# Prompt mixing rebuilt: four tiles projected at once in split fp32r, through DRAM, with key and query norms as scalars

## The chip, the cores and the metric

The kernel runs on one core of a Trainium2 chip. The time is that of one execution on the device, in microseconds (us). TensorE is called PE here (its weight loads PEld), VectorE DVE, ScalarE ACT, GpSimd POOL; SP is the engine that issues the DMAs.

## The reference, cut to what matters

One layer is computed for 2048 prompt positions and for 8 short running streams with the same weights. Here it is the mixing of the prompt that matters:

```python
h = rms_norm(x, norm1)
p = h @ w_in                      # 1024 -> 3080: u_A v_A q k v_B z (512 each), beta 4, a 4
y_a = gmlp_spatial(gelu(u_a), gelu(v_a), ...)        # 4 groups, blocks of 128 positions, then a norm per group
qkv_c = silu(causal_conv(qkv))    # depthwise, width 4
q = l2norm(q) * DK ** -0.5        # 4 heads of 128
k = l2norm(k)
g = -exp(a_log) * softplus(a + dt_bias); beta = sigmoid(b)
o, S = gated_delta_chunked(q, k, v, g, beta, S0, chunk)  # S_t from S_{t-1}: the tiles follow one another
y_b = rms_norm(o, gdn_norm) * silu(z)
x = x + concat(y_a, y_b) @ w_o    # from here on: the output phase
x = x + (silu(h2 @ w_gate) * (h2 @ w_up)) @ w_down
```

In a chunk the delta rule needs the inverse of a unit lower triangular matrix T, whose entries are beta, a decay exp(b_i - b_j) and k_i . k_j.

## The kernel before

Three stages follow one another: `mix_phase` for the sample streams, `mix_phase` for the prompt (16 tiles of 128 positions), `out_phase` (output projection and feed-forward, with every fp32 operand split into two fp32r halves and each product made of three). The first two keep the whole of w_in in SBUF (`w_in_sb`); `out_phase` takes the same region over.

In `mix_phase` each engine executes its own list, written out by hand, with semaphores between them; every engine executes strictly in its order. `tile(m, par, project, fronts)` handles tile m's recurrence and, in pieces between its products, the projection of tile m + 1: `qkv_columns`, `va_columns`, `z_columns`, `u_columns`, `gate_columns` (L960, L986 and L950), products in plain fp32 with 128 moving columns (512 for va). Per tile these are 160, 8 and 8. `project` is off for the last tile alone. Tiles 1 to 13 run in a loop of two tiles a turn.

A tile runs so on PE. `start` (L1011, L1012) sums the decays over partitions in fp32r with the constants `after_r` and `ones_r`, and likewise the squares of k and q. ACT turns these into `decay`, `eb`, `r_k` and `r_q` with Exp and Ln (L457 to L470), DVE makes the normalised `kn` and `qn` (L693, L695). `products` turns v and k to rows (L1043, L1048) and forms k . k and k . q (L1052, L1057); DVE makes `mt`, the masked matrix, of them (L708). Six doubling levels then build the inverse X and its transpose (`level_lx` L1081, `level_xlx` L1095 and L1099), each with a copy on ACT (L491), two updates on DVE (L735, L742) and a masked copy on POOL (L376). `scan` solves for delta (L1148), `outputs` and `state` follow, and `out_norm` (L1189) sums the squares of the output over partitions. ACT makes a reciprocal root of that sum, and DVE the scaled output. Between them ACT changes its function table (ACT_TABLE_LOAD): Silu, Gelu, and Exp with Ln lie in three different sets.

The convolution is done on DVE per tile in pieces of 128 columns (`conv_tap`, L677 and L679), and DVE splits the squares into halves (L755).

## Time and profile before

| | |
|---|---|
| time, median of 3 runs (lowest to highest) | 3163.26 us (3154.65 to 3163.99) |
| profiled execution: its span; its own time is not listed apart | 3160.3 us |
| PE busy, PEld, DVE, ACT | 97%, 91%, 44%, 30% of the span |
| sample mixing, prompt mixing, output phase | to 135.5, to 1361.8, to 3160.3 us |
| granted PE clock, mean | 0.982 of full |

The span runs from the first to the last instruction; the median of the runs is 2.96 us above it. Busy time says what an engine executed, not what it was waited for: for that one reads the instructions in order of time and looks at what ended the idle time before each. A 128-column fp32 product shows as two records, so "x16" of them are eight products. The ends of PE's records are modelled and overlap the next one's start; what a product costs is the distance between starts.

### The profile page before, as it was taken

How to read it: one execution, taken by the hardware profiler on the slowest of the kernel's cores; microseconds unless marked ns; L12 is line 12 of the kernel's file. 1: busy time of each engine (PE TensorE's matmuls, PEld its weight loads, DVE VectorE, ACT ScalarE, POOL GpSimd, SP SyncE). 2: the span in 40 equal slices, each digit the busy share in tenths (PEclk: the TensorE clock that was granted, in tenths of full speed). 3: DMA queues.
4: the chain of work that ended last, by engine and by line, in shares of the span. 5: the costliest groups of instructions: out<-in, count | busy, mean ns of one | idle time of the engine just before them, and what ended most of it. 6: DMA issues, size and time to landing. Idle time of an engine off the chain costs nothing.

```text
span 3160.3 us, 49318 instructions
## 1 busy us (share of the span) xinstructions
PE 3059.0 (97%) x20376; PEld 2869.0 (91%) x20376; DVE 1395.4 (44%) x2574; ACT 951.1 (30%) x1598; POOL 160.4 (5%) x155
## 2 busy tenths in 40 slices
PE   7799999999999999989999999999999999999998
PEld 6599999999899999879999999999999999999998
DVE  3255555454554554535343333453333435444344
ACT  3133433344443343324112112332112114322222
POOL 2001111111111111100000000000000000000000
PEclk9699999999999999989999999999999999999999
DMA  5100000000000000142221221521222215222220
GB/s 203 56 8 15 15 15 14 15 14 15 28 15 15 14 14 8 68 130 67 67 66 53 66 66 53 174 76 58 66 63 66 58 53 174 81 80 71 75 80 33
DMA packets 188615, 182.15 MB, mean 58 GB/s; under 512 B 5697, under 2 KB 162438, under 8 KB 188473
## 3 DMA queue, kind: packets, MB, share of 16 engines
q1 hardware_dynamic: 188472, 180.01, 18.3%
q8 instruction: 120, 1.97, 0.3%
q14 instruction: 23, 0.18, 0.0%
HBM read 159.37 MB, written 20.61 MB: 57 GB/s over the span
## 4 chain that ended last, share of the span: by engine, by line
PE 53%; DVE 2%; ACT 1%; issue 1%; DMA 0%; DVEq 0%; POOL 0%; ACTq 0%; POOLq 0%
PE gate_ps L1751 6%; PE gate_ps L1753 6%; PE gate_ps L1752 6%; PE up_ps L1751 6%; PE up_ps L1752 6%; PE up_ps L1753 6%; PE down_ps L1752 5%; PE down_ps L1751 5%; PE down_ps L1753 5%; DVE w_in_sb L1690 0%; ACT h_hi L1584 0%; DVE w_in_sb L1745 0%; DVE w_in_sb L1684 0%; DMA w_in_sb<-mixed_tiles 0%; ACT h_hi L1549 0%
## 5 line engine op out<-in xcount | busy, mean ns | idle before, releaser
L960 PE MATMUL pr_p<-hT_p,w_in_sb 128*128 128x128 f32 x5120 | 646.2, 280 | 0.8 <-DVE hT_p L618 0.8
L960 PEld LDWEIGHTS pr_p<-hT_p,w_in_sb 128*128 128x128 f32 x5120 | 608.5, 194 | 5.2 <-DVE hT_p L618 1.2
L1751 PE MATMUL gate_ps<-h_hi,w_hi 128*128 128x384 f32 (+1 forms) x1056 | 345.8, 327 | 3.7 <-DVE h_lo L1696 3.5
L1753 PE MATMUL gate_ps<-h_hi,w_lo 128*128 128x384 f32 (+1 forms) x1056 | 345.5, 327 | 0.0
L1752 PE MATMUL gate_ps<-h_lo,w_hi 128*128 128x384 f32 (+1 forms) x1056 | 345.3, 327 | 0.0
L1751 PE MATMUL up_ps<-h_hi,w_hi 128*128 128x384 f32 (+1 forms) x1056 | 344.3, 326 | 0.0
L1752 PE MATMUL up_ps<-h_lo,w_hi 128*128 128x384 f32 (+1 forms) x1056 | 344.0, 326 | 0.0
L1753 PE MATMUL up_ps<-h_hi,w_lo 128*128 128x384 f32 (+1 forms) x1056 | 344.0, 326 | 0.0
L1634 DVE TENSOR_TENSOR w_in_sb<-up_ps,w_in_sb 128x384 f32<-128x384 f32 (+1 forms) x132 | 70.7, 535 | 598.1 <-PE up_ps L1753 598.1
L1646 DVE TENSOR_TENSOR w_in_sb<-down_ps,w_in_sb 128x1024 f32<-128x1024 f32 x187 | 228.7, 1223 | 182.8 <-PE down_ps L1753 182.8
L1751 PE MATMUL down_ps<-wd_hi,act_hi 128*128 128x512 f32 x748 | 291.6, 390 | 2.2 <-DVE w_in_sb L1646 2.2
L1752 PE MATMUL down_ps<-wd_lo,act_hi 128*128 128x512 f32 x748 | 291.7, 390 | 0.0
L1753 PE MATMUL down_ps<-wd_hi,act_lo 128*128 128x512 f32 x748 | 291.6, 390 | 0.0
L1541 ACT ACTIVATE act_hi<-w_in_sb 128x384 fp32r<-128x384 f32 (+1 forms) x132 | 67.1, 508 | 530.2 <-DVE w_in_sb L1634 530.2
L1624 DVE TENSOR_TENSOR w_lo<-w_in_sb,w_hi 128x2048 fp32r<-128x2048 f32 x78 | 178.5, 2289 | 63.9 <-ACT w_hi L1530 63.9
L1751 PEld LDWEIGHTS gate_ps<-h_hi,w_hi 128*128 128x128 f32 x1056 | 199.4, 189 | 5.6 <-issue 4.4
L1752 PEld LDWEIGHTS gate_ps<-h_lo,w_hi 128*128 128x128 f32 x1056 | 199.3, 189 | 1.2
L1753 PEld LDWEIGHTS gate_ps<-h_hi,w_lo 128*128 128x128 f32 x1056 | 199.1, 189 | 0.0
L1751 PEld LDWEIGHTS up_ps<-h_hi,w_hi 128*128 128x128 f32 x1056 | 198.3, 188 | 0.0
L1752 PEld LDWEIGHTS up_ps<-h_lo,w_hi 128*128 128x128 f32 x1056 | 198.3, 188 | 0.0
L1753 PEld LDWEIGHTS up_ps<-h_hi,w_lo 128*128 128x128 f32 x1056 | 198.3, 188 | 0.0
L376 POOL TENSOR_TENSOR lt_p<-mt_p,link 128x512 f32<-128x512 f32 x96 | 137.5, 1439 | 1061.4 <-DVE mt_p L708 725.9
(370 smaller groups left out, 4661.5 us busy)
## 6 DMA issues: line engine op xcount, KB each, us to landing
w_in_sb<-in_w_gate SPq DMA_DIRECT2D x66, 512.0 KB, 3.9
w_in_sb<-in_w_up SPq DMA_DIRECT2D x66, 512.0 KB, 5.2
w_in_sb<-in_w_down SPq DMA_DIRECT2D x33, 1024.0 KB, 4.9
w_in_sb<-in_w_o SPq DMA_DIRECT2D x24, 512.0 KB, 6.4
w_in_sb<-in_w_in SPq DMA_DIRECT2D x5, 2048.0 KB, 15.7
w_in_sb<-mixed_tiles SPq DMA_DIRECT2D x17, 512.0 KB, 4.2
out<-w_in_sb SPq DMA_DIRECT2D x17, 512.0 KB, 4.1
xf_p<-in_x_prompt SPq DMA_DIRECT2D x16, 512.0 KB, 4.4
```

The source lines that it names most:

```text
L376: pool.tensor_tensor(lt[:, l % 2], mt[:], over_heads(sh["link"][:, l + 1, :]), ALU.mult)\
L960: last = pe.matmul(bank_[:, c * P:(c + 1) * P], sh["w_in"][:, k, col + c * P:col + (c + 1) * P], hT[:, par, k], start=(k == 0), stop=(k == ...
L1541: act_e.activation(act_hi[:, c, h * half:(h + 1) * half], act[:, h, 0:half], ACT.Copy)\
L1624: dve.tensor_tensor(w_lo[:, c], wraw[:, c], w_hi[:, c].bitcast(F32), ALU.subtract)\
L1634: dve.tensor_tensor(act[:, h, 0:half], up_ps[h][:, 0:half], gate_act[:, h, 0:half], ALU.mult)\
L1646: dve.tensor_tensor(acc[:, t, :], down_ps[t % 2][:].rearrange("p a b -> p (a b)"), acc[:, t, :], ALU.add).then_inc(added[t], 1)
L1751: pe.matmul(out, w_h, x_h, start=start, stop=False)
L1752: pe.matmul(out, w_h, x_l, start=False, stop=False)
L1753: return pe.matmul(out, w_l, x_h, start=False, stop=stop)
```

## The change

`mix_phase` is kept for the sample streams. The prompt gets a function of its own, `prompt_phase`. All loops in it are written out.

- The projection goes by items: one of 25 blocks of 128 columns of w_in (`ORDER`), for four tiles at a time (`MACRO`), with 512 moving columns. An item is 8 blocks of the inner dimension times three fp32r products (`three`), and stands in four quarters (`quarter`). The weights are not kept: SP loads each block again for each round of four tiles (100 loads of 512 KB), ACT makes the high half, DVE the low half. The normalised input of the round, hT, is split once per round (`split_h`). The 8 gate columns are the last 128 columns of w_in, as an item.
- ACT copies an item's result out of PSUM. Convolution is done on 512 positions at once, with 3 carried over in `halo`. SP stores each result to a DRAM tensor `stream_tiles`, and loads it back per tile: 20 blocks as `rc`, in two buffers, the four of z as `z`, in one.
- A slot is one tile of the recurrence (slots 0 to 15), with 25 quarters between its steps. Four slots, -4 to -1, come first with quarters alone; the items end with slot 11, so slots 12 to 15 have none.
- SiLU and GELU are applied to the loaded streams at the end of a slot, for the next tile (`silu_z`, `silu_streams`, `gelu_streams`).
- The key norm is folded into scalars per row: four squares with sums on ACT (`key_norms`), its inverse into beta, its root into the rows of v. The query norm is folded into the norm of the output: the squares of q times a constant are added by one product to the sum of the output's squares. The four sums of squares of k and q before, and the normalised kn and qn, go.

```diff
+STREAMS = [(x, c) for x in ("k", "q", "v", "va", "u", "z") for c in range(4)]
+ORDER = [("k", 0), ("ba", 0), ("k", 1), ("u", 0), ("k", 2), ("u", 1), ("k", 3), ("va", 0), ("q", 0), ("u", 2), ("q", 1),
+         ("va", 1), ("q", 2), ("va", 2), ("q", 3), ("va", 3), ("v", 0), ("v", 1), ("v", 2), ("v", 3), ("u", 3),
+         ("z", 0), ("z", 1), ("z", 2), ("z", 3)]
+MACRO = 4
+EARLY = 20
+RING_W = 3
...
+            def load_weights(n):
+                if n < ITEMS:
+                    past(sp, s["w_lo_ready"], n - 1)
+                    col = column[ORDER[n % NI]]
+                    sp.dma_start(wraw[:, n % 2], w_dram[:, :, col:col + P]).then_inc(raw_loaded[n % 2], 16)
+
...
+            def quarter(n, part):
+                if part == 0:
+                    load_weights(n + 3)
+                if part == 3:
+                    if 1 <= n <= ITEMS and kind(n - 1) == "plain":
+                        store_stream(n - 1)
+                    if 2 <= n <= ITEMS + 1 and kind(n - 2) == "conv":
+                        store_stream(n - 2)
...
+            def split_weights(n):
+                if n < ITEMS:
+                    act.wait_ge(raw_loaded[n % 2], 16 * (n // 2 + 1))
+                    past(act, s["item_done"], n - RING_W + 1)
+                    act.activation(w_hi[:, n % RING_W], wraw[:, n % 2], ACT.Copy).then_inc(s["w_hi_ready"], 1)
+
+            def split_h(j):
+                past(act, s["item_done"], j * NI)
+                for k in range(KC):
+                    act.wait_ge(s["hraw_ready"], 2 * MACRO * (j + 1))
+                    act.activation(hT_hi[:, k], hraw[:, k], ACT.Copy).then_inc(s["hT_hi_ready"], 1)
...
+            def quarter(n, part):
+                if part == 0 and n % NI == 0 and n < ITEMS:
+                    split_h(n // NI)
+                if part == 1:
+                    split_weights(n + 2)
+                if part == 2 and 1 <= n <= ITEMS:
+                    keep_item(n - 1)
...
+            def silu_streams(t):
+                act.wait_ge(rc_loaded[t % 2], 16 * (t // 2 + 1))
+                act.activation(rc[:, t % 2, 0:12], rc[:, t % 2, 0:12], ACT.Silu).then_inc(s["silu_ready"], 1)
+
+            def silu_z(t):
+                act.wait_ge(z_loaded, 16 * (t + 1))
+                act.activation(z[:], z[:], ACT.Silu).then_inc(s["z_ready"], 1)
+
+            def gelu_streams(t):
+                act.activation(rc[:, t % 2, 16:20], rc[:, t % 2, 16:20], ACT.Gelu_apprx_tanh).then_inc(s["u_ready"], 1)
+                act.wait_ge(s["va_turned"], t + 1)
+                past(act, s["sa_pe"], t)
+                act.activation(va[:], gs_cols, ACT.Gelu_apprx_tanh).then_inc(s["va_ready"], 1)
...
+            def key_norms(t):
+                act.wait_ge(s["k_turned"], t + 1)
+                past(act, s["root_k_ready"], t)
+                for h_ in range(H_B):
+                    if h_ > 0:
+                        act.wait_ge(s["ssk_ready"], t * H_B + h_)
+                    act.activation(junk[:], heads[1][:, h_], ACT.Square, accum_out=k_norm[:, 0, h_:h_ + 1])\
+                       .then_inc(s["ssk_ready"], 1)
+                act.wait_ge(s["ssk_ready"], (t + 1) * H_B)
+                act.activation(k_norm[:, 1], k_norm[:, 0], ACT.Ln, bias=sh["eps"][:]).then_inc(s["ln_k"], 1)
+                act.wait_ge(s["ln_k"], t + 1)
+                past(act, s["beta_n_ready"], t)
+                act.activation(k_norm[:, 2], k_norm[:, 1], ACT.Exp, scale=-1.0).then_inc(s["inv_k_ready"], 1)
...
+            def slot(t):
+                j = (t + MACRO) // MACRO
+                if t >= 0:
+                    decays(t)
+                    upto(t, 2)
+                    key_norms(t)
+                    upto(t, 4)
+                    scaled_values(t)
+                    query_squares(t)
+                    upto(t, 7)
+                    copy_x(t)
...
+                upto(t, SLOT)
+                if t >= 0:
+                    act.preload_act_table_set("silu_and_others")
+                    silu_z(t)
+                if t + 1 >= 0 and t + 1 < TILES:
+                    silu_streams(t + 1)
+                    gelu_streams(t + 1)
+                exp_and_ln()
...
+            def three(out, w_h, w_l, x_h, x_l, start, stop):
+                pe.matmul(out, w_h, x_h, start=start, stop=False)
+                pe.matmul(out, w_h, x_l, start=False, stop=False)
+                return pe.matmul(out, w_l, x_h, start=False, stop=stop)
+
+            def quarter(n, part):
+                if n >= ITEMS:
+                    return
+                if part == 0:
+                    pe.wait_ge(s["w_lo_ready"], n + 1)
+                    if n >= 2:
+                        what = {"conv": "kept", "ba": "ba_ready", "plain": "plain_ready"}[kind(n - 2)]
+                        pe.wait_ge(s[what], nth(n - 2) + 1)
+                w = n % RING_W
+                for k in (2 * part, 2 * part + 1):
+                    if n % NI == 0:
+                        pe.wait_ge(s["hT_lo_ready"], KC * (n // NI) + k + 1)
+                    last = three(pr[n % 2][:], w_hi[:, w, k], w_lo[:, w, k], hT_hi[:, k], hT_lo[:, k],
+                                 k == 0, k == KC - 1)
+                if part == 3:
+                    last.then_inc(s["item_done"], 1)
+
...
+            def slot(t):
+                j = (t + MACRO) // MACRO
+                if t >= 0:
+                    decays(t)
+                    upto(t, 1)
+                    turn_keys(t)
+                    upto(t, 2)
+                    keys_keys(t)
+                    upto(t, 3)
+                    turn_values(t)
+                    keys_queries(t)
+                    upto(t, 6)
+                if (t + MACRO) % MACRO == 1 and j < MACROS:
...
+                for l in range(LV):
+                    upto(t, 8 + 2 * l)
+                    if t >= 0:
+                        level_lx(l, t)
+                        if l == 0:
+                            keys_state(t)
+                    upto(t, 9 + 2 * l)
+                    if t >= 0:
+                        level_xlx(l, t)
+                        if l == 1:
+                            gmlp_norm(t)
+                    if l in (1, 3) and fronted(t) is not None:
+                        turn_h(l // 2, fronted(t))
+                upto(t, 21)
+                if t >= 0:
+                    solve(t)
+                    upto(t, 22)
+                    outputs(t)
+                    state(t)
+                    upto(t, 24)
+                    output_norm(t)
+                upto(t, SLOT)
+                if 0 <= t + 1 < TILES:
+                    turn_va(t + 1)
+
+            pe.wait_ge(s["set_masks"], 1)
+            for m in range(MACRO):
+                turn_h(0, m)
+                turn_h(1, m)
...
-            mix_phase(nc, shared, dict(
-                x=x_prompt, y=scratch[0:n_prompt], new_gdn=gdn_prompt[0, 0], new_conv=conv_prompt[0, 0],
-                ahead=loads_ahead(bufs, x_tiles, scratch, w_o), **weights), False)
+            prompt_phase(nc, shared, region, dict(
+                x=x_prompt, y=scratch[0:n_prompt], new_gdn=gdn_prompt[0, 0], new_conv=conv_prompt[0, 0], rec=streams,
+                ahead=loads_ahead(bufs, x_tiles, scratch, w_o), **weights))
```

At the end of a tile and the start of the next PE's list before holds this (`pr` are projection banks, `gb` banks of the recurrence, `ones` the constant that sums the squares of the output in X):

```order
L939 MATMUL pr_p<-ident,staging_p 128x128 x4
L960 MATMUL pr_p<-hT_p,w_in_sb 128x128 x8
L1189 MATMUL gb_p<-X_p,ones 128x512
...
L939 MATMUL pr_p<-ident,staging_p 128x128 x4
L960 MATMUL pr_p<-hT_p,w_in_sb 128x128 x8
...
L1011 MATMUL gb_p<-g_upto_p,after_r 128x512
L1012 MATMUL gb_p<-g_upto_p,after_r 128x512
...
L960 MATMUL pr_p<-hT_p,w_in_sb 128x128 x17
```

After the change, from slot 2 to slot 3 (`gb_p<-g_upto_p` are the decays, `gs_p<-ident` the turn of va, the last row the turn of the keys):

```order
L2291 MATMUL gb_p<-sq_q_p,eps_q_p 128x512
L2293 MATMUL gb_p<-X_p,ones 128x512
L2113 MATMUL pr_p<-hT_hi_p,w_hi_p 128x512
L2114 MATMUL pr_p<-hT_lo_p,w_hi_p 128x512
L2115 MATMUL pr_p<-hT_hi_p,w_lo_p 128x512
...
L2170 MATMUL gs_p<-ident,w_in_sb 128x128 x4
L2174 MATMUL gb_p<-g_upto_p,after_r 128x512
...
L2113 MATMUL pr_p<-hT_hi_p,w_hi_p 128x512
L2114 MATMUL pr_p<-hT_lo_p,w_hi_p 128x512
...
L2188 MATMUL gb_p<-ident,w_in_sb 128x128 x4
```

Two quarters of six split products, one on either side of the turn of va and the decays, stand where a column block (x8), the square sums and 32 column products with 8 gate products between them stood ahead of the first turn.

ACT's list at the same place before, from the reciprocal root of the output's squares on:

```order
L457 ACTIVATE r_k_p<-gb_p,eps 128x512
L460 ACTIVATE r_k_p<-r_k_p 128x512
L452 ACT_TABLE_LOAD
L452 ACTIVATE u_p<-pr_p 128x512
L394 ACT_TABLE_LOAD
L467 ACTIVATE decay_p<-gb_p 128x512
L470 ACTIVATE eb_p<-gb_p 128x512
```

and after, from slot 2 to slot 3 (the first row ends that root, then a weight split and a copy out of PSUM, then z, the twelve blocks of k, q and v, then u and va):

```order
L1720 ACTIVATE r_p<-r_p 128x512
L1647 ACTIVATE w_hi_p<-w_in_sb 128x1024
L1661 ACTIVATE w_in_sb<-pr_p 128x512
L1825 ACT_TABLE_LOAD
L1708 ACTIVATE z_p<-z_p 128x512
L1704 ACTIVATE w_in_sb<-w_in_sb 128x1536
L1711 ACT_TABLE_LOAD
L1711 ACTIVATE w_in_sb<-w_in_sb 128x512
L1714 ACTIVATE va_p<-gs_p 128x512
L1641 ACT_TABLE_LOAD
L1725 ACTIVATE decay_p<-gb_p 128x512
L1728 ACTIVATE eb_p<-gb_p 128x512
```

The squares' roots r_k and r_q leave; the silu of all streams and a table load more now stand between the root and the exponentials of the decays.

## Rows read from the trace of the kernel before

**Rows 1.** The page: span of the execution

```profile
span 3160.3 us, 49318 instructions
```

**Rows 2.** The stage: busy us of PE, PEld, DVE, ACT, POOL; granted clock, DMA

```profile
135.47:1361.76 1226.29, 1184.99 (x9424) 1100.59 (x9424) 607.95 (x1717) 482.36 (x980) 141.91 (x105) 0.98 0.06 19
```

**Rows 3.** POOL in order of time: first mask product, tiles 1 and 14

```profile
282.86 1.68 POOL L376 TENSOR_TENSOR lt_p<-mt_p,link 128x512 f32<-128x512 f32 x1 [42.94 <-DVE mt_p L708]
...
1251.46 3.46 POOL L376 TENSOR_TENSOR lt_p<-mt_p,link 128x512 f32<-128x512 f32 x2 [42.86 <-DVE mt_p L708]
```

**Rows 4.** PE in order of time inside a tile: start, us, what

```profile
741.27 1.95 PE L960 MATMUL pr_p<-hT_p,w_in_sb 128*128 128x128 f32 x16
743.05 1.00 PE L1095 MATMUL gb_p<-LX_p,XT_p 128*128 128x64 f32 x8
743.90 1.05 PE L1099 MATMUL gb_p<-XT_p,LX_p 128*128 128x64 f32 x8
```

**Rows 5.** PE in order of time, end of a tile and start

```profile
787.22 1.02 PE L1189 MATMUL gb_p<-X_p,ones 128*128 128x512 f32 x2
788.08 0.60 PE L939 MATMUL pr_p<-ident,staging_p 128*128 128x128 f32 x4
...
790.22 0.48 PE L1011 MATMUL gb_p<-g_upto_p,after_r 128*128 128x512 f32 x1
790.54 0.40 PE L1012 MATMUL gb_p<-g_upto_p,after_r 128*128 128x512 f32 x1
...
801.55 0.60 PE L1043 MATMUL gb_p<-ident,silu_v_p 128*128 128x128 f32 x4
```

**Rows 6.** PE in order of time, split products of the output phase

```profile
2160.57 0.39 PE L1751 MATMUL down_ps<-wd_hi,act_hi 128*128 128x512 f32 x1
...
2171.90 0.39 PE L1753 MATMUL down_ps<-wd_hi,act_lo 128*128 128x512 f32 x1
```

**Rows 7.** ACT in order of time around the end of a tile

```profile
788.34 0.69 ACT L457 ACTIVATE r_k_p<-gb_p,eps 128x512 f32<-128x512 f32 x1 [2.13 <-PE gb_p L1189]
...
789.71 1.28 ACT L452 ACT_TABLE_LOAD   x1
791.00 0.60 ACT L452 ACTIVATE u_p<-pr_p 128x512 f32<-128x512 f32 x1
```

**Rows 8.** Order of time, the last tile, with no projection beside it

```profile
1306.73 1.02 PE L1189 MATMUL gb_p<-X_p,ones 128*128 128x512 f32 x2
...
1315.59 1.12 PE L1048 MATMUL gb_p<-ident,knq_p 128*128 128x128 f32 x4 [1.80 <-DVE knq_p L693]
...
1318.46 1.13 DVE L708 SCALAR_TENSOR_TENSOR mt_p<-gb_p,beta_p,decay_p 128x128 f32<-128x128 f32 x4 [0.26 <-PE gb_p L1052]
...
1335.45 1.04 PE L1196 MATMUL pr_p<-ident,tails_p 128*3 128x128 f32 x8
...
1336.76 1.00 PE L1081 MATMUL gb_p<-X_p,lt_p 128*128 128x64 f32 x8
...
1353.29 1.08 PE L1189 MATMUL gb_p<-X_p,ones 128*128 128x512 f32 x2
...
1361.76 0.10 POOL L1516 MEMSET eps_b<- 128x1 f32 x1 [22.58 <-POOLq L87]
```

**Rows 9.** Granted clock (eighth value) in 2 us pieces of that tile

```profile
1314.00:1316.00 2.00, 0.41 (x2) 0.41 (x3) 0.69 (x1) 1.94 (x4) 0.00 (x0) 0.65 0.67 223
...
1324.00:1326.00 2.00, 2.00 (x17) 2.00 (x16) 1.07 (x2) 0.21 (x1) 0.10 (x1) 0.79 1.04 413
```

**Rows 10.** Group by line and shape: a 1024-element DVE operation

```profile
L1668 DVE TENSOR_TENSOR h_lo<-w_in_sb,h_hi 128x1024 fp32r<-128x1024 f32 x17 | 20.8, 1223 | 15.5 <-ACT h_hi L1549 15.4
```

**Rows 11.** PE in order of time, the start of the stage

```profile
142.47 1.11 PE L939 MATMUL pr_p<-ident,staging_p 128*128 128x128 f32 x4 [14.08 <-DVE staging_p L611]
...
146.27 1.01 PE L960 MATMUL pr_p<-hT_p,w_in_sb 128*128 128x128 f32 x3 [0.78 <-DVE hT_p L618]
```

**Rows 12.** DMA issues: KB each, median us to landing

```profile
xf_p<-in_x_prompt SPq DMA_DIRECT2D x16, 512.0 KB, 4.4
```

More of the change, by code:

```diff
@@ L1299, in _, with stream_columns @@
                 turn_tails()
+def stream_columns():
+    names = [("k", 2 * D_A + D_B), ("q", 2 * D_A), ("v", 2 * D_A + 2 * D_B), ("va", D_A), ("u", 0), ("z", 2 * D_A + 3 * D_B)]
+    return {(x, c): col + c * P for x, col in names for c in range(4)}
+STREAMS = [(x, c) for x in ("k", "q", "v", "va", "u", "z") for c in range(4)]
+ORDER = [("k", 0), ("ba", 0), ("k", 1), ("u", 0), ("k", 2), ("u", 1), ("k", 3), ("va", 0), ("q", 0), ("u", 2), ("q", 1),
+         ("va", 1), ("q", 2), ("va", 2), ("q", 3), ("va", 3), ("v", 0), ("v", 1), ("v", 2), ("v", 3), ("u", 3),
+         ("z", 0), ("z", 1), ("z", 2), ("z", 3)]
@@ new lines, with prompt_buffers @@
+MACRO = 4
+EARLY = 20
+RING_W = 3
+def prompt_buffers(region):
+    KC = D_MODEL // P
+    flat = region[:].rearrange("p c n -> p (c n)")
+    taken, views = 0, {}
+    for name, shape, axes in (
+            ("hraw", (KC, MACRO * P), "p (a b) -> p a b"),
+            ("wraw", (2, KC, P), "p (a b c) -> p a b c"),
+            ("cin", (2, 4 + MACRO * P), "p (a b) -> p a b"),
+            ("conv", (2, MACRO * P), "p (a b) -> p a b"),
+            ("plain", (2, MACRO * P), "p (a b) -> p a b"),
+            ("ba", (MACRO * P,), None),
+            ("xf", (D_MODEL,), None),
+            ("h", (D_MODEL,), None),
+            ("spare", (504,), None),
+            ("rc", (2, EARLY, P), "p (a b c) -> p a b c"),
+            ("yT", (KC, P), "p (a b) -> p a b"),
+            ("lt", (2, H_B, P), "p (a b c) -> p a b c"),
+            ("LX", (LEVELS_OF[P], H_B, P), "p (a b c) -> p a b c"),
+            ("kq_eb", (2, H_B, P), "p (a b c) -> p a b c"),
+            ("v_rows", (H_B, P), "p (a b) -> p a b"),
+            ("k_dec", (H_B, P), "p (a b) -> p a b")):
+        n = math.prod(shape)
+        view = flat[:, taken:taken + n]
+        if axes:
+            view = view.rearrange(axes, **dict(zip("abcd", shape)))
+        views[name] = view
+        taken += n
+    return views
@@ L1857, in _, with stream_step @@
                     block_of(b, g, gi, n)
-def stream_step(nc, t, outs, scratch):
+def stream_step(nc, t, outs, scratch, streams):
     y_prompt, y_sample, gdn_prompt, conv_prompt, gdn_sample, conv_sample, v_sample = outs
@@ L1903 @@
     scratch = nc.dram_tensor("mixed_tiles", (tiles, P, D_MODEL), F32, kind="Internal").ap()
-    stream_step(nc, tensors, outs, scratch)
+    streams = nc.dram_tensor("stream_tiles", (SEQ // P, P, len(STREAMS) * P), F32, kind="Internal").ap()
+    stream_step(nc, tensors, outs, scratch, streams)
     result = run_bass_kernel_spmd(nc, [arrays], core_ids=[0]).results[0]
```

746 lines of the change are left out of this document (added).

## The prediction

> **What bounds the kernel now.** I first read the page for the span, 3160.3 us [rows 1], then split it by stages. Prompt mixing runs from 135.47 to 1361.76, 1226 us, and PE is busy for 1185 of them at 0.98 of full clock; DVE has 608, ACT 482 [rows 2]. What comes before and after is not touched, so only these 1226 us can move. PE bounds them: the pace of a tile is (1251.46 - 282.86) / 13 = 74.5 us [rows 3], and in the order of time one group of products starts where the last ends: eight 128-column products take 1.78 us (741.27 to 743.05), four 64-column ones 0.85 [rows 4], a 512-column fp32 product 0.86 (787.22 to 788.08) [rows 5]. So the question is what PE executes afterwards, and where it starts to wait.
>
> **PE's own work.** Projection of one tile before: 160 products at 0.22 = 35.6, eight of 512 columns at 0.86 = 6.9, eight small ones for the gates at 0.14 to 0.22, together about 44 us, 703 for 16 tiles. After: 100 items (four rounds of 25 column blocks) of 24 split products with 512 columns. The output phase has just these, 50 in 2171.90 - 2160.57 = 11.33, 0.227 each [rows 6]: 5.44 us an item, 544 in all. That is 159 us less. The rest of a tile, added up for the new order: 17 groups of the solve at 0.86, 14.7; six groups of four 128-column products at 0.89, 5.3; eight for the output, 1.8; six times four transposes at 0.45 (0.60 in [rows 5] with the modelled drain), 2.6; six fp32r products of 512 columns, 1.6; two fp32 ones for the output norm, 1.7. That is 27.7 us, and before it was 27.9 by the same prices (the four square sums go, one fp32 product for the query norm comes). A quarter item follows fp32 work some 21 times a slot, and the first fp32r product after fp32 took 0.32 against 0.227 [rows 5, 6]: 1.9 us a slot. A slot with projection beside a tile is therefore 25 x 1.36 + 1.9 + 27.7 = 63.6 us of dense PE. Were that all, twelve such slots would give back 131 us. It isn't all, in three places.
>
> **The start of a slot.** In the new order PE has, after the product that sums the output squares (call its end T), one quarter item, a turn, the two decays, one quarter item, and then the turn of the keys: 1.4 + 0.45 + 1.0 + 1.4 = 4.3 us. That turn waits for silu and for eb, the exponential of the second decay product. Before, PE had from 788.08 to 801.55, 13.5 us of work, between that sum and the first product that waits on the decays [rows 5]. What ACT does between T and eb, in its order: 0.26 until Ln starts (788.08 to 788.34) and 1.37 for Ln and Exp [rows 7]; splits and copies of two quarters, 0 to 1.65, mean 0.8; a table load 1.30 (789.71 to 791.00); silu of z 0.6; silu of 1536 elements, 1.5 as an estimate from 0.60 for 512 at 0.83 per thousand more; a table load 1.30; gelu of u and of v, 1.1; a third load 1.30; two exponentials, 1.1. Sum 10.7. PE idles 10.7 - 4.3 = 6.4 us, twelve times, 77 us. No other engine can hide it, since PE executes in order, and behind the turn stand all the slot's items.
> The row shows a table load of 1.28 us with the next operation 0.01 behind it [rows 7]. The Trainium skill (ScalarE: Activation LUTs, What ACT_TABLE_LOAD costs) puts some 1380 ns of drain beside the 1283 of the load, 2.66 us a switch. By its figure three loads a slot would add 4.1 us to each of sixteen slots, 66 us. The trace has the load's length but no drain, and I take the row.
>
> **The clock.** In the last tile PE had 0.41 us of work in 1314 to 1316 and its granted clock fell (0.65 of that piece at full), and was back only in 1324 to 1326 (0.79) [rows 9], 1.2 GHz in between. At the start of the stage dense work began at 146.27 [rows 11]. An idle stretch of 6.4 us is longer than that one, so I let the clock fall at each slot's start. Dense PE gets it back sooner than the sparse last tile did; I take 4.6 us at half speed, which costs 2.3, with 0 and 5 (the whole 10 us of that row) as bounds. Twelve slots: 28 us.
> Slots 4 and 8 also split a new round of h just there (eight ACT passes of 0.6, DVE behind each with 0.7, after DVE's masked decay and its product of 1024 elements, 1.22 [rows 10]): the first quarter waits until T + 12.6, an idle 9.7 in place of 6.4; slot 0 likewise, 75 us. In slots 1, 5 and 9 the gate sums wait for DVE, which takes the gates after gmlp: 2 us each. Slots 8 to 11 turn no h, 0.9 less each.
>
> **No cover in the last four tiles.** Before, one tile ran without projection: 1306.73 to 1353.29, 46.6 us [rows 8], against 27.7 of work. Now there are four, since items end after slot 11. Such a tile changes so: the keys are turned at T + 9.9 (the sum above without the 0.8) where 1315.59 is T + 8.0 (T = 1306.73 + 0.86), +1.9; the masked key products began 2.9 later (1318.46) [rows 8] and now wait for four squares with sums, Ln and Exp on ACT and beta on DVE, about 4.2, +1.3; a second fp32 product in the output norm, +0.9; twelve turns of tails go, -1.3 (1335.45 to 1336.76). 49.4 us, four times 198.
>
> **The sum.** The first tile's h is with PE at 142.47, 7.0 after the stage began, of which 4.4 is a landing [rows 11, 12]; three more tiles cost 4.4 + 2.6 each, turning 3.8 (to 146.27), the first split 1.3: 168.5. Then 25 items alone: 136, with four turned tiles 3.5, a cold start 2.3, gates 0.7: 311. Slots 0 to 11: nine at 63.6 + 6.4 + 2.3 = 72.3, one 75, two 75.6, + 6 - 3.5: 879, ends at 1190, its T at 1189. Four bare tiles: 1387. From T to the first instruction of the output phase as before, 1361.76 - 1354.15 = 7.6 [rows 8]: 1394.5, 33 us later than 1361.76. Span 3160.3 + 33 = 3193; the runs' median, 3163.26, is 3.0 above the profiled span, which holds for both: **3196 us**.
> The total agrees: 544 of items, 16 x 27.7 of tiles less 4 of turned h, 23 of switches, 92 of waits at starts and gates, 28 of clock, 4 x 21.7 of idle in bare tiles, 33 before the first item, 3 of its cold start and gates, 7.6 at the end: 1257 against 1226, +31. (Before, the same prices give 1188 of the 1226; the rest is edges of its loop and waits that I don't price, and is no term of the new sum.)
> Edits costed at nothing, with their cover: splitting weights (ACT 1.05, DVE 1.22 [rows 10]) and convolution (four DVE passes, 2.9) per item, 4.1 of DVE against 5.44 alone and 10 to 11 beside a tile; if a DVE pass were 40% longer the first round would be bound by it, +25. Weight blocks of 512 KB are issued about seven quarters before ACT needs them, 9.5 us in the first round, against 4.4 landing for the same size [rows 12]; streams go out at 256 KB an item and come back as 1.3 MB a tile, asked for some 12 us or more before use.
>
> **Rivals.** (1) The wait at the slot's start is covered, and PE is simply dense: it decides if ACT reaches eb within 4.3 us of T. Then 12 x 8.7 = 104 go: 3092, faster. For it speaks PE's 97% now; against it that ACT's list is strict and each length measured. 9%. (2) The waits come, but the clock stays up: -28, 3168, no change. The granted clock did fall in the last tile, yet behind a longer sparse stretch. 11%. (3) SP is the late one: it issues in order, and its waits for the taps of an item two back stand ahead of the next weight load; DVE passes those taps only after eb. If weights come late by one landing a slot less the slack, some 4 us: +48, 3244. Against: seven quarters of lead. 13%. (4) A switch of tables holds ACT for longer than its row, for a second time the 1.28 us of [rows 7]: three a slot, sixteen slots, +61, 3257. The row speaks against it, 0.01 us from the load's end to the next operation. 3%. The rule that would give it is the one of ScalarE: Activation LUTs in the Trainium skill, named above. My forecast, waits at the slots' starts and bare tiles as summed, holds 64%.
>
> **Numbers.** Own range of the forecast 3165 to 3230: clock 0 to 5 a slot (-28, +32), switches 0 to 23, bare tiles +-3 each. A difference under 0.3% (9.5 us, 3153.8 to 3172.7) can't be told from none here. Slower: 57 of the forecast's 64, all of (3), (4): 73. Same: 5 of the forecast, 7 of (2): 12. Faster: 2 of the forecast, 4 of (2), (1): 15. For 8 in 10 the range runs from 3140 to 3250: it leaves out (1), (4) and a little at both ends.
>
> **What the profile would show.** Right: split products 0.227 apart; an idle of PE of about 6 us ended by ACT's eb in each of slots 0 to 11, PEclk under 1.0 behind it; a pace of 72 to 73 us; four tiles near 49 us at the end; the output phase beginning near 1394. Wrong: PE waiting for the low half of the weights (then 3), no idle at the turn of the keys (1), an idle over 9 us there (4).

## The result, and the profile after

The changed kernel takes 3187.47 us (median of 4 runs, 3186.41 to 3196.89), the one before 3163.62 (4 runs on the same chip, 3154.65 to 3166.32): 1.0093 times as long by the estimate over all runs, 95% interval [1.0078, 1.0108]; the two medians alone give 1.0075. It is slower, by more than 0.3%. The profiled span grew from 3160.3 to 3184.9, by 24.6 us; 33 were forecast.

The page of the kernel after: the span, and the weight blocks' loads, which are new in this stage.

```profile
span 3184.9 us, 41999 instructions
...
w_in_sb<-in_w_in SPq DMA_DIRECT2D x100, 512.0 KB, 4.4
```

The mixing stage as one window: length, busy time (with counts) of PE, its weight loads, DVE, ACT and POOL, then the clock, DMA share and GB/s.

```profile
135.47:1387.00 1251.53, 1072.11 (x6180) 923.32 (x6180) 627.49 (x1160) 520.80 (x1006) 146.61 (x105) 0.92 0.35 101
```

Against [rows 2] PE has 1072 us of work where it had 1185, in a stage that lasts 25 us longer and at a clock of 0.92, not 0.98. So the projection did become cheaper, and more than all of it was lost to idle time and a slow clock. The waits of PE in the stage by what ended them (total, times, longest) say where; the fourth line is ACT's, for weight blocks:

```profile
PE gb_p L2188 <- ACT eb_p L1728: 90.3, 13, 8.4
...
PE gs_p L2146 <- DVE w_in_sb L1899: 27.5, 4, 18.3
PE pr_p L2113 <- DVE hT_lo_p L1854: 27.0, 4, 9.4
...
ACT w_hi_p L1647 <- DMA w_in_sb<-in_w_in: 10.9, 2, 6.3
```

The first is the turn of the keys waiting for eb: nine slots and the four bare tiles (slots 12 to 15, which have no items beside them). The second is the start of the stage. The third holds slots 0, 4 and 8 (6.15, 9.43, 9.43; the other 1.99 is the first item). ACT's two waits for weights, 6.33 and 4.55, lie at 143 and 230 us, in the first round, and PE never waits for a weight's low half. One slot's start, in slot 7, on PE:

```profile
820.31 1.02 PE L2293 MATMUL gb_p<-X_p,ones 128*128 128x512 f32 x2
820.77 0.79 PE L2113 MATMUL pr_p<-hT_hi_p,w_hi_p 128*128 128x512 f32 x1
...
822.56 0.60 PE L2170 MATMUL gs_p<-ident,w_in_sb 128*128 128x128 f32 x4
...
823.70 0.39 PE L2175 MATMUL gb_p<-g_upto_p,ones_r 128*128 128x512 f32 x1
...
825.09 0.40 PE L2115 MATMUL pr_p<-hT_hi_p,w_lo_p 128*128 128x512 f32 x1
832.50 1.09 PE L2188 MATMUL gb_p<-ident,w_in_sb 128*128 128x128 f32 x4 [7.01 <-ACT eb_p L1728]
...
835.94 1.53 PE L2194 MATMUL gb_p<-w_in_sb 128*128 128x128 f32 x8
```

and the same time on ACT:

```profile
821.43 0.69 ACT L1718 ACTIVATE r_p<-gb_p,eps_o_p 128x512 f32<-128x512 f32 x1 [4.83 <-PE gb_p L2293]
822.15 0.63 ACT L1720 ACTIVATE r_p<-r_p 128x512 f32<-128x512 f32 x1
822.68 1.05 ACT L1647 ACTIVATE w_hi_p<-w_in_sb 128x1024 fp32r<-128x1024 f32 x1
823.63 0.58 ACT L1661 ACTIVATE w_in_sb<-pr_p 128x512 f32<-128x512 f32 x1
824.23 1.28 ACT L1825 ACT_TABLE_LOAD   x1
825.53 0.63 ACT L1708 ACTIVATE z_p<-z_p 128x512 f32<-128x512 f32 x1
826.06 1.47 ACT L1704 ACTIVATE w_in_sb<-w_in_sb 128x1536 f32<-128x1536 f32 x1
827.55 1.28 ACT L1711 ACT_TABLE_LOAD   x1
...
829.97 1.28 ACT L1641 ACT_TABLE_LOAD   x1
831.27 0.60 ACT L1725 ACTIVATE decay_p<-gb_p 128x512 f32<-128x512 f32 x1
831.76 0.59 ACT L1728 ACTIVATE eb_p<-gb_p 128x512 f32<-128x512 f32 x1
```

ACT never rests between the output norm's Ln and eb, and PE is idle for 7.01 of those 11 us. The windows in the wait (the first row) and behind it show the clock (eighth value):

```profile
828.00:831.00 3.00, 0.00 (x0) 0.00 (x0) 0.70 (x2) 2.97 (x4) 0.00 (x0) 0.85 0.73 178
832.50:835.00 2.50, 2.50 (x8) 2.20 (x9) 2.36 (x6) 1.28 (x8) 0.00 (x0) 0.50 0.20 82
835.00:837.00 2.00, 2.00 (x9) 1.72 (x8) 0.46 (x2) 1.94 (x7) 0.00 (x0) 0.52 0.00 0
837.00:839.00 2.00, 2.00 (x13) 1.68 (x13) 1.97 (x3) 0.28 (x1) 0.00 (x0) 1.00 0.00 0
```

PE works at 0.50, which is 1.2 GHz, for some 4 us after the wait, and at 2.4 GHz again from 837. The turn of `va` stands right behind the last quarter of a slot, so its starts count slots (the ends of round 0 and of slot 11), and in the bare tiles it stands at the end of the output norm's sum:

```profile
313.78 0.60 PE L2170 MATMUL gs_p<-ident,w_in_sb 128*128 128x128 f32 x4
...
1187.14 0.60 PE L2170 MATMUL gs_p<-ident,w_in_sb 128*128 128x128 f32 x4
1235.10 0.60 PE L2170 MATMUL gs_p<-ident,w_in_sb 128*128 128x128 f32 x4
1282.98 0.60 PE L2170 MATMUL gs_p<-ident,w_in_sb 128*128 128x128 f32 x4
```

Twelve slots take 1187.14 - 313.78 = 873.4, 72.8 each, where [rows 3] had 74.5 a tile; a bare tile takes 47.9. The output phase begins at 1387.36.

### The profile page after: what moved, and what is told of

It is laid out like the page before. It is cut to its first block, busy times and chain, and to the rows that moved or that the text cites. A ratio compares the mean times of both kernels' runs of the same rounds, so it can differ in the third digit from the quotient of the medians.

```text
span 3184.9 us, 41999 instructions
## 1 busy us (share of the span) xinstructions
PE 2944.1 (92%) x17132; PEld 2689.4 (84%) x17132; DVE 1414.9 (44%) x2017; ACT 989.7 (31%) x1624; POOL 164.9 (5%) x156
## 4 chain that ended last, share of the span: by engine, by line
PE 53%; DVE 2%; ACT 1%; issue 1%; DVEq 0%; POOL 0%; ACTq 0%; POOLq 0%
PE gate_ps L2804 6%; PE gate_ps L2806 6%; PE gate_ps L2805 6%; PE up_ps L2806 6%; PE up_ps L2804 6%; PE up_ps L2805 6%; PE down_ps L2804 5%; PE down_ps L2805 5%; PE down_ps L2806 5%; DVE w_in_sb L2743 0%; ACT h_hi L2637 0%; DVE w_in_sb L2737 0%; DVE w_in_sb L2798 0%; ACT w_hi L2583 0%; ACT h_hi L2602 0%
## 5 line engine op out<-in xcount | busy, mean ns | idle before, releaser
L2113 PE MATMUL pr_p<-hT_hi_p,w_hi_p 128*128 128x512 f32 x800 | 347.4, 434 | 27.0 <-DVE hT_lo_p L1854 27.0
L2687 DVE TENSOR_TENSOR w_in_sb<-up_ps,w_in_sb 128x384 f32<-128x384 f32 (+1 forms) x132 | 70.7, 536 | 597.6 <-PE up_ps L2806 597.6
L2115 PE MATMUL pr_p<-hT_hi_p,w_lo_p 128*128 128x512 f32 x800 | 320.7, 401 | 0.0
L2114 PE MATMUL pr_p<-hT_lo_p,w_hi_p 128*128 128x512 f32 x800 | 319.4, 399 | 0.0
L1848 DVE TENSOR_TENSOR w_lo_p<-w_in_sb,w_hi_p 128x1024 fp32r<-128x1024 f32 x100 | 122.5, 1225 | 187.9 <-ACT w_hi_p L1647 187.9
L2113 PEld LDWEIGHTS pr_p<-hT_hi_p,w_hi_p 128*128 128x128 f32 x800 | 156.1, 195 | 55.3 <-issue 31.5
```

What stands on the lines that cost most here:

```text
L1848: dve.tensor_tensor(w_lo[:, n % RING_W], wraw[:, n % 2], w_hi[:, n % RING_W].bitcast(F32), ALU.subtract)\
L2113: pe.matmul(out, w_h, x_h, start=start, stop=False)
L2114: pe.matmul(out, w_h, x_l, start=False, stop=False)
L2115: return pe.matmul(out, w_l, x_h, start=False, stop=stop)
L2687: dve.tensor_tensor(act[:, h, 0:half], up_ps[h][:, 0:half], gate_act[:, h, 0:half], ALU.mult)\
```

## The experiments

Ratios are to the kernel before unless another is named. That kernel was run again beside each group of experiments, with medians from 3161.25 to 3164.42, so a difference in us to the changed kernel's 3187.47 is good to some 3 us. Line numbers are those of each kernel's own source.

**dummy_fill: the clock alone.**

```diff
+            def fill(t, count):
+                past(pe, s["ln_o"], t)
+                for i in range(count):
+                    pe.matmul(gb[4][:], sh["ones_r"][:], flat(g_upto[:, 0]), start=True, stop=True)
...
                     decays(t)
+                    if t in (0, 4, 8):
+                        fill(t, 24 if t == 0 else 38)
                     upto(t, 1)
+                    if t < 12 and t % 4:
+                        fill(t, 24)
                     turn_keys(t)
```

> The idle stretch of TensorE at the start of slots 0 to 11 is filled with products that nobody reads (512 columns, fp32r, into a free bank): 24 of them, 5.5 us, before the turn of the keys, and 38 before the first quarter in slots 4 and 8. The wait itself stays as long as it is. Theory (the granted clock falls in the idle stretch and the 4 us at half speed behind it cost 2.0 us a slot): clock stays at 1.00 behind the wait, 12 x 2.0 = 24 us less than the changed kernel's 3187.5, about 3163. Rival (the slow stretch lies under other waits and costs nothing): 3187.

3170.27 us, ratio 1.0025 [1.0013, 1.0037]: 17.2 below the changed kernel by the medians. The profiled span is 3162.2, 22.7 below; it is the fastest of ten runs (up to 3178.04). Behind a remaining wait of 1.42 us the clock reads 1.00 (windows from slot 7's turn of the keys):

```profile
817.90:820.40 2.50, 2.46 (x16) 2.23 (x17) 2.36 (x6) 1.67 (x9) 0.00 (x0) 1.00 0.26 105
```

The keys are turned no sooner: 817.93 is 10.35 behind ACT's last exponential of the output norm (807.58), and so was 832.50 behind 822.15. PE only does useless work meanwhile. In the two profiled executions all of the difference lies in the twelve slots: the last sum of squares starts at 1377.89 and at 1355.32. So the clock's aftermath is worth 22.7 us there, and 17 by the medians. It isn't spread evenly. From sum to sum slots 3, 7 and 11 gave back only 0.43 to 0.46 each, slot 0 3.9, the other eight 1.5 to 2.4. In slots 3, 7 and 11, at full clock, PE waits 0.62 for XT and 1.29 for the attention mask, where the changed kernel has 0.64 or less for the two: what the clock had cost there was nearly all covered.

**no_tables: ACT's list, and the price of a table load.**

```diff
-                act.activation(z[:], z[:], ACT.Silu).then_inc(s["z_ready"], 1)
+                act.activation(z[:], z[:], ACT.Copy).then_inc(s["z_ready"], 1)
...
-                    act.preload_act_table_set("silu_and_others")
...
-                exp_and_ln()
```

(and so for the streams' silu and both gelus).

> Silu and gelu are replaced by a copy of the same size (the nonlinearity is left out), so the three table loads at the end of a slot go and nothing else on ScalarE does. Theory (a load costs its row, 1.28 us, and the chain to eb sets PE's wait): eb 3.9 us earlier, wait 3.0 in place of 7.0; 12 x 3.9 = 47 and four bare tiles x 3.9 = 16, about 3125, or about 3100 if the clock stays up behind the shorter wait. Rival (a switch holds ScalarE a second time as long): eb 7.8 us earlier, the wait gone, 12 x 7 + 24 of clock + 4 x 7.8 = 139 less, about 3048. Rival (the wait is not set by ScalarE's list but by the weights): 3187.

3115.41, ratio 0.9849 [0.9827, 0.9871]: 72 us below the changed kernel. Its waits on PE, and slot 7 on ACT:

```profile
PE gb_p L2186 <- ACT eb_p L1728: 38.9, 13, 4.1
...
PE pr_p L2111 <- DVE hT_lo_p L1852: 15.7, 4, 5.2
```

```profile
788.67 0.69 ACT L1718 ACTIVATE r_p<-gb_p,eps_o_p 128x512 f32<-128x512 f32 x1 [4.82 <-PE gb_p L2291]
...
794.25 0.59 ACT L1725 ACTIVATE decay_p<-gb_p 128x512 f32<-128x512 f32 x1
796.08 0.60 ACT L1728 ACTIVATE eb_p<-gb_p 128x512 f32<-128x512 f32 x1 [1.23 <-DVE w_in_sb L2043]
```

Ln to the decays' exponential is 5.6 us, where it was 831.27 - 821.43 = 9.8: 4.2 less, the three loads' 3.84 and a little overlap. A second price on each load, the fourth rival, would have made it 7.7 less. The two waits together fell by 62.7 us, and the mean clock rose from 0.960 to 0.968; that the clock accounts for the rest of the 72 was not measured apart. A second limit shows instead: eb shares its buffer with the normed output, and now waits 1.23 us for VectorE to read it.

**small_weights: are the weights late?**

```diff
-                sp.dma_start(wraw[:, n % 2], w_dram[:, :, col:col + P])...
+                    c = slice(0, KC if n < 2 else 1)
+                    sp.dma_start(wraw[:, n % 2, c], w_dram[:, c, col:col + P])...
```

> Each load of a weight block from the third on moves an eighth of it, 64 KB in place of 512 (so most products use the first blocks' weights); all waits and all other work stay. Theory (weight loads land before anyone waits for them): 3187, within 3 us. Rival (SyncE's in-order queue brings the weights late, some 4 us a slot, or their traffic slows other engines): about 3140, with the waits of the splits shorter.

3191.41, ratio 1.0093 [1.0069, 1.0117]; 45 of the page's 284 MB are gone, and nothing else:

```profile
PE gb_p L2189 <- ACT eb_p L1729: 90.3, 13, 8.4
```

The same 90.3. So the size of the weight loads costs nothing. This run keeps SP's order and its waits, so it doesn't test whether SP issues a load late; that half of the third rival is settled by the changed kernel's own waits, none of PE's for a low half and two of ACT's for a block, both in the first round.

**fp32_items: does PE set the projection's pace?**

```diff
-                    last = three(pr[n % 2][:], w_hi[:, w, k], w_lo[:, w, k], hT_hi[:, k], hT_lo[:, k], ...)
+                    last = pe.matmul(pr[n % 2][:], w_hi[:, w, k].bitcast(F32), hT_hi[:, k].bitcast(F32), ...)
```

> The changed kernel with one fp32 product in place of each three split ones (the low halves are left out of the product, the split work stays): eight products of 0.86 an item, 6.9 us in place of 5.44. Theory (TensorE's products set the pace of the projection): 100 x 1.44 = 144 more, 23 less for the switches between fp32 and fp32r that go, 12 x 0.7 less wait at the slots' starts: 3187 + 113, about 3300. Rival (the splits, the convolution or the weights set the pace of an item): under 3250.

3303.36, ratio 1.0451 [1.0434, 1.0469]: +116 on the changed kernel. It is the one number here that checks the product prices and the switches together.

**no_eps_product: the query norm's price.**

```diff
-                pe.matmul(gb[4][:], eps_q[:], flat(sq_q[:]), start=True, stop=False)
```

> The changed kernel without the fp32 product of 512 columns that brings the query norm into the output norm (the query's part of that norm is left out). Theory (it stands on TensorE's own path in every tile, 0.86 us): 16 x 0.86 = 14 less, 3187 - 14 = about 3173. Rival (ScalarE's list sets the start of a slot, and the list starts behind the output norm's product, so nothing is hidden): the same. Rival (TensorE waits there anyway): 3187.

3173.64 in seven runs, ratio 1.0029 [1.0016, 1.0042], 13.8 less, as sixteen times 0.86 would have it; 3187 is ruled out. Tile by tile the traces don't bear the sum out. In the profiled executions the twelve slots are 13.2 us shorter in all, 0.2 in slot 0 and 3.4 in slot 9, and the four bare tiles only 0.24 in place of 3.4. The product is gone there, but the clock fell ahead of the last sum (6.84 us up to it in the third bare tile, the changed kernel first):

```profile
1323.17:1330.01 6.84, 5.00 (x37) 4.23 (x36) 1.08 (x4) 1.74 (x5) 0.00 (x0) 1.00 0.01 2
```

```profile
1309.56:1316.40 6.84, 5.61 (x29) 5.31 (x29) 0.00 (x0) 1.74 (x5) 0.00 (x0) 0.55 0.00 0
```

So the total fits, but the product's own price isn't shown apart from changes of the clock, and the close agreement is in part luck.

**eb_first: half of ACT's list.**

```diff
-        o_norm = eb
+        o_norm = sq_a
...
                 if t >= 0:
+                    if t + 1 < TILES:
+                        decays(t + 1)
                     act.preload_act_table_set("silu_and_others")
-                    silu_z(t)
                 if t + 1 >= 0 and t + 1 < TILES:
                     silu_streams(t + 1)
+                if t >= 0:
+                    silu_z(t)
```

> Order on ScalarE alone: the two exponentials of the next tile's decays go ahead of the table switch, and the streams' silu ahead of z's; the normed output gets a buffer of its own so that eb is free early. The turn of the keys then waits for the silu: 0.26 + 1.37 + 0.8 + 1.1 + 1.3 + 1.5 = T + 6.4 against 4.3 us of cover. Theory (that list is what TensorE waits for): wait 2 to 2.6 us in place of 5.6 to 7.0, 12 x 4.3 = 52 less, 4.2 less in each of four bare tiles = 17, about 3118; if the clock doesn't fall behind so short a wait, 24 less again, about 3094. Rival (something else is ready just as late as eb was): 3180 or more.

3170.27, ratio 1.0027 [1.0015, 1.0039]: 17 less, not 69. PE's waits in the stage, and slot 7 on PE:

```profile
PE gb_p L2194 <- ACT w_in_sb L1704: 35.6, 13, 3.9
PE gb_p L2219 <- DVE XT_p L1977: 32.4, 10, 5.9
```

```profile
820.80 0.66 PE L2194 MATMUL gb_p<-ident,w_in_sb 128*128 128x128 f32 x4 [2.55 <-ACT w_in_sb L1704]
834.68 0.78 PE L2219 MATMUL gb_p<-ident,XT_p 128*128 128x128 f32 x4 [2.53 <-DVE XT_p L1977]
```

The wait at the keys fell to 2.55 as forecast. But gelu and two table loads still stood ahead of the key norms on ACT, so XT was as late as ever, and PE waited for it at the turn of X. The wait had a second station that the first one had covered: of 55 us gained at the keys 24 came back there (the changed kernel has some 8 at that place, in the bare tiles) and 5 at other places; the last 8 or 9 between these and the 17 I can't place. The clock also fell behind the 2.55: 0.64 in 820.80 to 823.00, 0.54 in 823.00 to 825.00.

**cover: quarters ahead of the keys.**

```diff
                     decays(t)
-                    upto(t, 1)
+                    upto(t, (4, 3, 2, 4)[t % 4])
                     turn_keys(t)
```

> Order on TensorE alone: one to three of the slot's quarters (2.3 on the mean, 3.1 us) stand before the turn of the keys instead of between it and the turn of X; ScalarE and VectorE as before. Theory now, after eb_first moved the wait to the turn of X (key norms, scaled key products and XT follow the turned keys in a chain of some 10 us): the quarters only change places, the waits for eb shrink by 3.1 a slot and come back at the turn of X; 3180 to 3190. Theory of the prediction (the wait at the turn of the keys is all there is): 12 x 3.1 = 37 less, about 3150.

3182.7, ratio 1.0069 [1.0052, 1.0085], 5 less than the changed kernel and hardly to be told from it. The waits for eb fell from 90.3 to 65.9, and half of that came back at the turn of X, where it had been some 8:

```profile
PE gb_p L2188 <- ACT eb_p L1728: 65.9, 13, 8.4
...
PE gb_p L2213 <- DVE XT_p L1971: 20.9, 11, 4.2
```

Waits for the attention mask, the gates and the copies out of PSUM took some 6 more, which leaves about the 5 that were gained. So the start of a slot is one chain, from the output norm's sum over eb, keys, key norms and masked products to X, and PE's quarters in it can be spent once.

**moved: take the chain's head off the path.** ACT's two nonlinear phases go into the solve's levels, and PE issues the next tile's decays before the output norm:

```diff
+                        if l == 3:
+                            act.preload_act_table_set("silu_and_others")
+                            if nxt and not late:
+                                silu_streams(t + 1)
+                            else:
+                                silu_z(t)
+                        if l == 4 and nxt and not late:
+                            silu_z(t)
+                            gelu_u(t + 1)
+                        if l == 5:
+                            if nxt and late:
+                                silu_streams(t + 1)
+                                gelu_u(t + 1)
+                            if nxt:
+                                gelu_va(t + 1)
+                            exp_and_ln()
...
                     outputs(t)
                     state(t)
+                    if t + 1 < TILES:
+                        decays(t + 1)
```

(`late` are slots 3, 7 and 11, whose streams land later; the normed output has its own buffer as in eb_first, `va` is turned at level 4, and SyncE asks for a new round's streams after 13 quarters in place of 24.)

> The same work in another order: silu, gelu and their three table loads go from between two tiles into ScalarE's idle time in the solve's levels 3 to 5, the next tile's decays and their exponentials ahead of the output norm; the normed output has a buffer of its own. The keys are then turned a quarter after the output norm. Theory (TensorE's waits are those of ScalarE's list and the slow clock is their aftermath): 58 us of waits for eb in the slots, 33 in the bare tiles, 24 of clock and some 16 of 19 at the rounds' first quarters go: 3187 - 130, about 3057. Rival (dense slots run into another limit, as the chain of key norms to X): waits at the turn of X of some 5 us, about 3110.

3084.65, ratio 0.9753 [0.9737, 0.9769]: 103 below the changed kernel and 77 below the one before. Its largest waits on PE in the stage:

```profile
PE gs_p L2171 <- DVE w_in_sb L1920: 26.8, 4, 17.7
PE gb_p L2219 <- DVE sq_a_p L2062: 16.9, 9, 3.8
PE pr_p L2138 <- DVE hT_lo_p L1875: 12.9, 4, 6.3
...
PE gb_p L2238 <- DVE XT_p L1992: 9.9, 4, 3.1
```

No wait for eb is among them. Of the 27 us missing against the forecast 17 are the second row, a new wait for the last tile's normed output, which the products of keys with keys need out of their bank; slot 0 still waits 6.3 for its h where 3 were forecast. Behind these waits the clock falls again; what that costs was not measured apart.

**moved_h, kk_late, best, final: what is left.** moved_h splits a new round's h behind the quarters of the old round's last item; kk_late puts the products of keys with keys behind the values; best adds the query product in fp32r and buffers of their own for the first four x; final takes two of VectorE's quarters from in front of XT.

```diff
+                if part > 0 and n % NI == NI - 1 and n + 1 < ITEMS:      # moved_h, ACT and DVE
+                    split_h(n // NI + 1, (2 * part - 2, 2 * part - 1))
...
                     upto(t, 2)                                            # kk_late, PE
-                    keys_keys(t)
-                    upto(t, 3)
                     turn_values(t)
                     keys_queries(t)
+                    upto(t, 3)
+                    keys_keys(t)
...
-        sq_q = sb("sq_q", [P, H_B, P])                                   # best
+        sq_q = sb("sq_q", [P, H_B, P], F32R)
...
-                    upto(t, 4)                                            # final, DVE
+                    upto(t, 2)
                     products(t)
```

> As moved, and the split of a new round's h is begun while the old round's last item runs, two of eight column blocks behind each of its quarters. Theory: the three remaining waits for the low half of h (some 3 us each) go with their clock, 9 less than moved, about 3048. Rival (eight passes on ScalarE and VectorE beside the output norm delay that instead): as moved or a few us more.

> As moved_h, and the products of keys with keys, which wait for the last tile's normed output on VectorE, go behind the turn of the values and the products of keys with queries. Theory (the 19.8 us at that place, 3.8 in slots 2, 6 and 10, are a wait for the bank that other ready work can cover): some 16 less, with 3 or 4 us of clock, about 3064. Rival (the masked key products come later and X is turned late, or level 0 waits for POOL): as moved_h, 3082.

> As kk_late, with the query norm's product in fp32r (0.23 in place of 0.86 us) and the first four tiles of x loaded at once into buffers of their own, squared and normed without waiting for one another. Theory: 16 x 0.63 = 10 less, and the first item some 10 us earlier than 171: 20 less than kk_late, about 3044. Rival (the first item waits for its weights and the eight splits of h in any case): 10 less than kk_late.

> As best, and VectorE takes two quarters of the projection's passes (instead of four) ahead of the scaled key products and XT; the other two come behind them. In the trace of best VectorE works without a gap from 506 to 522 us, and TensorE waits 26.7 us in nine turns of X, some 17 of them in five slots. Theory (the chain key norms, key products, XT, X is late by the convolution passes ahead of it on VectorE): XT is 1.5 to 3.4 us earlier, some 14 of the 17 go, with 2 or 3 of clock: 3076 - 17, about 3059. Rival (the passes that come later delay the levels by as much, or the weights' low halves): 3070 to 3080.

| kernel | us | ratio to before | expected |
|---|---|---|---|
| moved | 3084.65 | 0.9753 [0.9737, 0.9769] | 3057 |
| moved_h | 3082.69 | 0.9746 [0.9730, 0.9763] | 3048 (9 under moved) |
| kk_late | 3087.58 | 0.9763 [0.9746, 0.9780] | 3064 |
| best | 3076.23 | 0.9719 [0.9702, 0.9736] | 3044 (20 under kk_late) |
| final | 3081.24 | 0.9741 [0.9728, 0.9755] | 3059 |

Only best can be told from its parent, 11 under kk_late: its first item begins at 162.73 (172.41 in kk_late, 170.96 in the changed kernel), 8 to 10 earlier, so of the 10 forecast for the query product little arrived. kk_late and final failed in the same way. The waits of PE at the first part of a tile, in kk_late and then in final (moved_h had 19.8 at the bank of keys with keys, 9.9 at XT):

```profile
PE gb_p L2247 <- DVE XT_p L1999: 26.8, 9, 3.9
...
PE gb_p L2254 <- DVE attn_p L2004: 5.0, 10, 1.3
```

```profile
PE gb_p L2267 <- DVE XT_p L2017: 19.1, 9, 3.9
PE gb_p L2274 <- DVE attn_p L2022: 18.7, 12, 3.9
```

Each order moved the wait: from keys with keys to XT, from XT to the attention mask. VectorE is what they share. In best it works from 506.25 to 522 without a gap of half a microsecond on weight splits, convolution, the state, masked decays, the last tile's normed output, and then the masked key products and XT; ahead of it it was idle for 12.22 us, waiting for ACT's half of a weight split. So it isn't short of time over a slot, only in this stretch of its list. final moved two quarters of its passes out and gained nothing; other passes were not tried.

## Why the prediction was right

**The sign and the mechanism** held, by its own steps: cheaper products, and more than their gain lost at the slots' starts, to the clock and in the bare tiles. Nine turns of the keys waited for eb inside the slots, 57.7 us (90.3 less the bare tiles' 7.48 and three times 8.36), and slots 0, 4 and 8 waited 25.0 for h: 82.7 where the steps have 6.4 x 9 + 19.4 and slot 0's 9, some 86.

**Products** (0.227, 5.44 an item, 159 us less): fp32_items, worked out from the same prices, was expected 113 above and measured 116.

**Switches** (0.09 each): a quarter's first product is followed after 0.31 us and the next ones after 0.23, as [rows 5, 6] had it. Of the runs only fp32_items tests them, together with the products.

**The wait at the keys** (6.4): 5.6 to 5.9 in slots 1, 5 and 9, 6.5 in slots 2, 6 and 10, 7.0 in slots 3, 7 and 11. The spread is the quarters' splits and copies, which the prediction had as 0.8 on the mean. In slot 7 the sum ended at 821.17 and eb at 832.35, 11.2 against 10.7. The estimate for silu of 1536 elements, 1.5, measured 1.47.

**Clock** (2.3 a slot, 28 in all): 22.7 in all by dummy_fill's profiled execution, 17 by its medians, so mis-sized by 5 to 11. One price for every slot was wrong too: 0.4 in slots 3, 7 and 11, 1.5 to 3.9 in the others.

**Start** (first item at 168.5, round 0's end 311): 170.96 and 313.78. The first tile's turn came at 146.91, 4.4 later than taken from [rows 11], because ACT waits for the first weight block (until 143.32) ahead of the first tile's norm; the next three came 6.1 apart in place of 7.0. **Slots in all** (879): 873.4. Of the 5.6 less, 4.3 are slot 0, which took 70.7 for 75 and waited 6.15 for h, not 9.1. **Bare tiles** (49.4): 49.3 for the first, 47.9 for the others, 193 in place of 198. The first is the longer one because its clock reads 0.60 in the 6.84 us up to its last sum, 1.00 in the other three; the prediction has no term for the clock there, and its 49.4 fits that tile by luck. The keys were turned 9.9 behind the sum as forecast (1330.87 to 1340.76); the masked key products came 13.5 behind it, not 14.1, and the other 0.9 I can't place. **From the last sum to the output phase** (7.6): 8.6, 1378.75 to 1387.36. The stage ends 7.1 us before the forecast's 1394.5: 2.8 lost at the start, 5.6 gained in the slots, 5 in the bare tiles, 1.0 lost at the end. The median is 8.5 below 3196, by mis-sized terms and not by a missing one.

**Rivals.** (1), covered starts, is ruled out by the 7.01 rows. (2), the clock stays up, by the 0.50 rows. (3), late weights, by the waits of the changed kernel and, for the size of the loads, by small_weights. (4), a dearer switch, by no_tables and by the rows: a load ends at 831.25 and the next exponential starts at 831.27. The Trainium skill (ScalarE: Activation LUTs, What ACT_TABLE_LOAD costs) adds a drain of some 1380 ns to each; the trace and the run disagree with it here.

**What the prediction did not see.** It took the turn of the keys for the only late point. eb_first and cover show that X is late at the same time, behind the same list: had someone removed only the wait that the trace names, 17 or 5 us would have come, not the 69 and 37 forecast from that wait alone.

## What to carry to other kernels

Before giving an in-order engine cheaper work, add up the chain that its neighbour runs between two of its stations, in that neighbour's own order with its table loads, and compare it with the work that is left as cover. When a wait is named in the trace, ask who would wait next if it were gone: taking its head and the table phases off it (moved, with a buffer and SyncE's earlier requests, 103 us) paid, removing one link or shifting the cover (eb_first 17, cover 5) hardly did. Phases on a table set of their own belong into stretches where that engine only copies; here the solve's levels took three loads and four functions.

## What the runs showed of the hardware

The granted clock fell after an idle stretch of 2.55 us (eb_first, 0.64 and 0.54 behind it), though it stayed at 1.00 behind one of 1.42 in dummy_fill, where the engine had been filled up to it; after idle stretches of 5.6 to 7.0 us about 4 us ran at 1.2 GHz. The length of one idle stretch doesn't decide it alone: in the bare tiles of no_eps_product the clock fell (0.55) around waits of 0.60 and 1.23, and behind the same two waits it stayed at 1.00 in the changed kernel.

An addition of 128x512 on VectorE that takes 0.69 us elsewhere took 1.67 beside a product of the same size on POOL, and a copy of three columns 1.26 where it otherwise takes 0.16 (slot 7 of the kernel after):

```profile
840.91 3.51 POOL L1633 TENSOR_TENSOR w_in_sb<-mt_p,link 128x512 f32<-128x512 f32 x2 [44.07 <-DVE mt_p L1964]
841.59 1.67 DVE L1971 TENSOR_TENSOR XT_p<-XT_p,ident 128x512 f32<-128x512 f32 x1
843.18 1.26 DVE L1863 COPY w_in_sb<-halo_p 128x3 f32<-128x3 f32 x1
```

The addition takes 1.63 to 1.67 in all sixteen tiles, and took 1.63 to 1.65 in the kernel before; the copy is slow in the six slots where it comes next. The addition stands on the chain to X, so a microsecond a tile goes with POOL's masks; that they cause it is read from the overlap and was not tested.
